# A Hymba-style encoder block with a hierarchical MoE on one core: the scatter of the pair before moves behind this pair's up matmuls

## The reference

```python
# 4 groups x 8 experts, d_model 1024, d_expert 512, all float32
h = h + mix @ w_o[l]
h = h + hier_moe(rms_norm(h, norm2_g[l]), w_group[l], b_group[l], w_expert[l], b_expert[l],
                 w_gate[l], w_up[l], w_down[l])
return rms_norm(h, final_g)
...
# hier_moe: top-1 group, then top-2 experts in it; combine holds the weight of each token and expert
for gi in range(N_GROUPS):
    h = jax.nn.silu(jnp.einsum('nd,edf->nef', xt, w_gate[gi])) * jnp.einsum('nd,edf->nef', xt, w_up[gi])
    y = y + jnp.einsum('nef,efd->nd', h * combine[:, gi, :, None], w_down[gi])
```

## Time and profile before

| what | value |
|---|---|
| runs | 638.72 us median of 3 (636.98 to 640.76) |
| profiled execution, span | 639.8 us; no time beside the span is given for it, and it lies within the runs |
| TensorE matmul busy | 593.8 us, 93% |
| TensorE weight load busy | 288.1 us, 45% |
| VectorE / ScalarE / GpSimd busy | 149.8 / 77.6 / 28.5 us |
| mean granted TensorE clock | 0.982 of full speed |
| read from HBM | 216.16 MB, 340 GB/s over the span |

### The profile page before, as it was taken

The page is one execution under the profiler, slowest core; times in us unless marked ns, Lnnn a source line. Parts: engine busy times, 40 slices in busy tenths (PEclk is TensorE's granted clock), DMA queues, the critical chain, the costliest instruction groups (busy, mean ns, idle before and its releaser), DMA issues.

```text
span 639.8 us, 6965 instructions
## 1 busy us (share of the span) xinstructions
PE 593.8 (93%) x2801; PEld 288.1 (45%) x2801; DVE 149.8 (23%) x331; ACT 77.6 (12%) x151; POOL 28.5 (4%) x60
## 2 busy tenths in 40 slices
PE   4999899959999999999999999999999999999984
PEld 2445657546535353544434343434353535344321
DVE  1006545251111111121213031211111111212023
ACT  2013323121000010101000101010000101010002
POOL 2031200210000000000000000000000000000001
PEclk9999989978999999999999999999999999999999
DMA  6995680073989999999999999999999999979701
GB/s 259 338 425 226 248 288 1 34 296 130 385 349 419 416 413 410 411 421 416 419 413 418 411 419 420 414 420 417 417 415 419 421 410 410 410 296 392 307 1 67
DMA packets 35939, 217.50 MB, mean 340 GB/s; under 512 B 5136, under 2 KB 6184, under 8 KB 28368
## 3 DMA queue, kind: packets, MB, share of 16 engines
q1 hardware_dynamic: 31680, 214.30, 82.3%
q10 hardware_dynamic: 4240, 2.94, 1.4%
HBM read 216.16 MB, written 1.06 MB: 340 GB/s over the span
## 4 chain that ended last, share of the span: by engine, by line
PE 91%; DVE 5%; issue 2%; DMA 1%; SPq 0%; ACT 0%; POOLq 0%; POOL 0%; DVEq 0%; ACTq 0%
PE bank L1188 33%; PE bank L1216 17%; PE bank L1175 10%; PE bank L1226 10%; PE bank L1003 7%; PE bank L1072 4%; PE bank L1062 2%; PE bank L1267 2%; DVE region_x L882 2%; PE bank L986 2%; PE bank L1040 1%; PE bank L1282 1%; PE bank L1051 1%; DMA ring<-in_norm_g_dram 1%; DVE region_q L886 1%
## 5 line engine op out<-in xcount | busy, mean ns | idle before, releaser
L1188 PE MATMUL bank<-ring,region_x 128*64 128x512 f32 x960 | 212.1, 594 | 0.6 <-issue 0.6
L1188 PEld LDWEIGHTS bank<-ring,region_x 128*64 128x64 f32 x960 | 75.0, 137 | 132.5 <-issue 132.5
L1216 PE MATMUL bank<-ring,region_q 128*64 128x512 f32 x480 | 106.3, 594 | 15.3 <-DVE region_q L886 8.7
L897 DVE TENSOR_TENSOR h<-h,bank 128x512 f32<-128x512 f32 x64 | 44.0, 687 | 238.2 <-PE bank L1226 238.2
L1216 PEld LDWEIGHTS bank<-ring,region_q 128*64 128x64 f32 x480 | 39.7, 137 | 72.2 <-issue 72.2
L1175 PEld LDWEIGHTS bank<-region_q,region_t 128*128 128x128 f32 x512 | 61.0, 199 | 14.0 <-issue 14.0
L1175 PE MATMUL bank<-region_q,region_t 128*128 128x128 f32 x512 | 64.0, 285 | 1.7 <-DVE region_q L878 1.7
L1226 PE MATMUL bank<-region_x,region_q 128*128 128x512 f32 x128 | 62.2, 618 | 0.7 <-ACT region_x L621 0.7
L1003 PE MATMUL bank<-ring,region_x 128*128 128x512 f32 x96 | 44.7, 622 | 0.8 <-DVE region_x L660 0.8
L1226 PEld LDWEIGHTS bank<-region_x,region_q 128*128 128x128 f32 x128 | 20.4, 188 | 42.4 <-DVE h L897 21.0
L621 ACT ACTIVATE region_x<-bank 128x512 f32<-128x512 f32 x32 | 19.1, 597 | 159.3 <-PE bank L1216 140.3
(11 more groups left out here) (156 smaller groups left out, 273.5 us busy)
## 6 DMA issues: line engine op xcount, KB each, us to landing
ring<-in_w_gate_dram SPq DMA_DIRECT2D x30, 2048.0 KB, 12.3
ring<-in_w_up_dram SPq DMA_DIRECT2D x29, 2048.0 KB, 12.2
ring<-in_w_down_dram SPq DMA_DIRECT2D x29, 2048.0 KB, 11.9
ring<-in_w_in_dram SPq DMA_DIRECT2D x8, 768.0 KB, 9.1
ring<-in_w_up_dram SPq DMA_DIRECT2D x12, 512.0 KB, 9.7
ring<-in_w_down_dram SPq DMA_DIRECT2D x12, 512.0 KB, 9.2
ring<-in_w_o_dram SPq DMA_DIRECT2D x2, 2048.0 KB, 8.6
ring<-in_w_gate_dram SPq DMA_DIRECT2D x8, 512.0 KB, 7.8
```

Of the source, the lines that this page charges most:

```text
L897: dve.tensor_tensor(part, part, ps[SC0 + k % 2][:], ALU.add).then_inc(sc_free, 1)
L1188: last = pe.matmul(ps[bank][64 * a:64 * a + 64, :], xgT[:, c, 64 * a:64 * a + 64], slots[s][:, c * F:(c + 1) * F], start=(c == 0), stop=(c ...
L1216: last = pe.matmul(ps[GD0 + half][64 * a:64 * a + 64, :], hT[:, c, 64 * a:64 * a + 64], w[:, c * D + 512 * half:c * D + 512 * half + 512], ...
```

## The change

On TensorE, a step's order becomes: gather of i (now in two calls of `gather_half`), pick transposes (`turn_picks`), down of i-1, gate of i, up of i, scatter of i-1, transposes of i. The transposes of a pair's activations thus stand at the end of the step before the one with its down; those of pair 0 follow its up ahead of the first step. The wait for the two gather copies ahead of down is split: the first half of down waits for ScalarE's, the second for VectorE's. On VectorE, the hT copy goes ahead of the GD1 copy, and the product ahead of the four adds. ScalarE's and SyncE's programs are unchanged.

```diff
@@ VectorE
             def pair_step(trip, j):
                 i = trip * BODY + (1 + j)
+                hT_out(trip * BODY + j)
                 gathered_out(i)
-                hT_out(trip * BODY + j)
                 dve.wait_ge(picks_turned, i + 1)
                 make_picks(trip * BODY + (2 + j), trip * BODY + (base + j + 1))
+                product(i)
                 add_outputs(trip * BODY + j)
                 places_out(i)
-                product(i)
...
+            hT_out(PAIRS - 2)
             gathered_out(PAIRS - 1)
-            hT_out(PAIRS - 2)
+            product(PAIRS - 1)
             add_outputs(PAIRS - 2)
             places_out(PAIRS - 1)
-            product(PAIRS - 1)
             hT_out(PAIRS - 1)
             add_outputs(PAIRS - 1)
@@ TensorE
-            def gather(i):
-                pe.wait_ge(pick_ready, i + 1)
-                for b in range(2):
-                    for c in range(4):
-                        for t in range(TT):
-                            last = pe.matmul(ps[GD0 + b][:, c * P:(c + 1) * P], hn[:, t, 4 * b + c, :], pick[:, t, :],
-                                             start=(t == 0), stop=(t == TT - 1))
-                    last.then_inc(gathered, 1)
+            def gather_half(i, b):
+                if b == 0:
+                    pe.wait_ge(pick_ready, i + 1)
+                for c in range(4):
+                    for t in range(TT):
+                        last = pe.matmul(ps[GD0 + b][:, c * P:(c + 1) * P], hn[:, t, 4 * b + c, :], pick[:, t, :],
+                                         start=(t == 0), stop=(t == TT - 1))
+                last.then_inc(gathered, 1)
+
+            def turn_picks(i):
                 if not isinstance(i, int) or i > 0:
                     pe.wait_ge(place_ready, i)
                 for t in range(TT):
...
-            def down(i, trip, f):
+            def down(i, trip, f, after):
                 pe.wait_ge(hT_ready, i + 1)
                 landed(pe, trip, f + 4)
                 landed(pe, trip, f + 5)
                 for half in range(2):
+                    pe.wait_ge((xg_act, xg_dve)[half], after + 1)
                     for c in range(FC):
...
-            gather(0)
+            gather_half(0, 0)
+            gather_half(0, 1)
+            turn_picks(0)
             products(0, 0, FIRST_FILL, GATE, gate_done, gate_pieces)
             products(0, 0, FIRST_FILL + 2, UP, up_done)
             pe.wait_ge(first_pieces_in, 16 * 2 * (PIECES - 1))
             pe.nop().then_inc(scattered, 4)
+            turn_act(0)
...
-                gather(i)
-                turn_act(before)
-                pe.wait_ge(xg_act, i + 1)
-                pe.wait_ge(xg_dve, i + 1)
-                down(before, trip, f - 6)
+                gather_half(i, 0)
+                gather_half(i, 1)
+                turn_picks(i)
+                down(before, trip, f - 6, i)
                 return i, before, f
 
             def whole_pair_step(trip, j):
                 i, before, f = pair_step(trip, j)
                 products(i, trip, f, GATE, gate_done)
+                products(i, trip, f + 2, UP, up_done)
                 scatter(before)
-                products(i, trip, f + 2, UP, up_done)
+                turn_act(i)
...
             last_product(0, GATE, gate_done)
+            last_product(1, UP, up_done)
             scatter(PAIRS - 2)
-            last_product(1, UP, up_done)
             turn_act(PAIRS - 1)
```

## The result

The changed kernel takes 618.37 us, the median of 4 runs (616.26 to 621.16), against 639.74 for the one before on the same chip: a ratio of 0.966 (0.963 to 0.970), 21 us less. The forecast was 622.2, with a range from 618.5. The direction and the bound are right; the gain is larger than the 16.6 us of the sum, and the median lies just under the range. What failed in the sum is the price of the gather in its new place, and in a small part that of down; this is taken up behind the experiments.

A forecast was written before the change was run, and what follows sets the result against it. TensorE's order of work was taken as the bound, idle between gather and down. Steps of 29.09 for 30.23 us gave 14.8, minus 0.2 first, plus 2.05 last: 16.6 less, 622.2 us median; own range 619.5 to 625.

The forecast's parts named there:

- the sum: Whole kernel: 14.8 us gained in thirteen steps, 0.2 lost in the first, 2.05 gained in the last; 16.6 less.
- the price of the gather in its new place: TensorE, each step: the gather was entered at 3.78 us in the step sum of 29.09.
- bounds for down: TensorE, down behind a pick transpose: between 6.87 and 7.09 us, entered at 7.09.
- shows no such seam: TensorE, gate to scatter: a second seam would give 0.15 us and a 28.94 step; left out of the sum.
- The low end of the range: Whole kernel: 619.5 us as own range, step 28.95; below it 618, with down at 6.87 and a shorter scatter.
- the 1.75 forecast: Last step, after the scatter: down waits 1.75 us for hT, behind the last add and L902 on VectorE.
- A: TensorE's transposes cost 0.67 and the sequencer's 0.34 stays ahead of down: 0.57 us a step, 630 us; chance 0.12.
- B: VectorE's product delays the scatter's adds if over 0.29 us later: 627 us at half its 0.69, 632 at all; chance 0.10.
- D: VectorE's hT copy comes late for down, beyond 2.6 us of margin: slower, 653 us at 4.8 us delay; chance 0.02.
- C: Weight loads set the pace as the ring runs short: 625 or 630 us, L273 standing for microseconds; chance 0.10.
- E: Loads already fill the step, idle time moves to L273: only the last step's 2.05 us gained, 636.7 median; chance 0.03.
- L273's 51 ns: Median wait for landed weights, taken as evidence against loads setting the pace; expected to stay at 51 ns.

The follow-up runs named there:

- third-bank version: The changed kernel with the scatter's third matmul writing the bank GATE, so only the fourth waits for an add of this pair: 615.58 us, ratio 0.961; again 615.44, 0.960.
- adds-first run: The changed kernel with VectorE's product behind the four adds and the copy L902, as before the change: 648.04 us, ratio 1.011.
- hT run: The changed kernel with VectorE's hT copy behind its GD1 copy, as before the change: 639.92 us, ratio 1.000.
- half-gather run: The changed kernel with the second block of 128 tokens left out of the gather, same loads: 609.87 us, ratio 0.954.
- product-late run: The kernel before, with only VectorE's product of a pair moved behind its GD1 copy for the next pair: 673.11 us, one run.

## Where the prediction was right, and the step of it that failed

**The bound** was read rightly: TensorE's order, with the idle place at down. The gap is now 0.22 as forecast, the transposes take 0.44, and the scatter 3.82. Four things had to be right at once for a step of 28.80. Each was taken back in a run of its own, and these are the prices a step: the split wait 0.8, hT ahead of the GD1 copy 1.3, the product ahead of the adds 1.9, the scatter as cover 1.2.

**The step that failed** is the pricing of the gather and of down in their new places. The prediction took the gather over at its 3.78, though it moved from behind up to behind transposes. The runs: the gather takes 3.78 behind up, with or without the product beside it, and 3.57 to 3.59 behind a scatter or transposes (but for the six of 3.65 to 3.71). That is 0.21 a step. Of its bounds for down, 6.87 and 7.09, the prediction took the upper. Down takes 7.02 behind running work and 7.09 only behind an idle time, another 0.07. Together they are what the step was short of, 29.09 - 28.80 = 0.29, in thirteen steps 3.8 us. With 0.2 in the first step and 0.3 in the last, the sum of 16.6 becomes 20.9, against 21.0 in the traces. The mechanism of the gain held; it was these two terms that had the wrong size.

**Why the gather's term was missed.** The seams are changes between 64-column and 128-column matmuls. Before, a step had four: ahead of down, of the scatter, of up and of the gather. The new order takes away those ahead of up (0.15) and of the gather (0.21). The prediction named only the first. It looked for the second ahead of the scatter, where the trace "shows no such seam", though in its own words the scatter stands behind a 64-column stream as before; the one that goes is the gather's. The rows of the gather's weight loads in the pages of the kernel before and of the changed one show it too, 14.0 us of idle time ahead of them for 1.9:

```profile
L1175 PEld LDWEIGHTS bank<-region_q,region_t 128*128 128x128 f32 x512 | 61.0, 199 | 14.0 <-issue 14.0
...
L1175 PEld LDWEIGHTS bank<-region_q,region_t 128*128 128x128 f32 x512 | 59.8, 196 | 1.9 <-issue 1.9
```

The two seams that stay have a price as well. Ahead of the scatter it is 0.20 by the third-bank version; that was measured behind up, and that it is as much behind gate follows only from the 3.82 that the scatter takes in either place. It moved with the scatter and changes no sum. Ahead of down it can be read from down's 7.02 against gate's 6.87, for as many records. The Trainium skill, TensorEngine Tiling (Array Packing), Key Properties, says that a change of tiling mode drains TensorE; the 3.78 and 3.57 of the gather, the 7.02 and 6.87 of up and the 3.63 of the scatter agree with it.

**Slips in the working.** The low end of the range was built on down at 6.87 and a scatter without 0.4 us of waits. These are 0.22 and 0.4 a step, 14 x 0.62 = 8.7, and would have put it near 613.5; the text takes 0.3 a step, half of it, and gives no reason. A step of 28.95 belongs to a time of some 620.3, not 619.5. Six of the thirteen steps before, not one in three, took 30.15; the sum, which goes by their mean, doesn't hang on that.

**First and last step.** The first took 30.29 for 30.49: 0.28 less by the gather and down, 0.09 more since the bare transposes of pair 0 hold up the gather by 1.49 and not 1.4. The last took 30.08 for 30.40, by the same 0.28; its wait for hT came out nearly as priced:

```profile
594.71 0.42 DVE region_q L902
595.12 0.61 DVE region_q L886
...
595.78 7.11 PE bank L1288 x32
```

The scatter ends at 594.08 and down starts 1.70 later, for the 1.75 forecast.

**The rivals.** A, dearer seams, went the other way: transposes behind the scatter cost 0.44. B would have needed 0.29 us: that is what VectorE idles between product and add, so the cover holds exactly as thin as priced. The adds-first run shows the price when the order on VectorE is wrong, larger than the 0.69 that I gave as the most for B, since there the transposes wait for all of the queue. D didn't come: hT is ready 2.6 us ahead of down. What a late hT costs is shown by the hT run, which loses just what the gain was. C was closer than its chance of 0.10 says. The loads do fall back 1.0 a step; by the estimates above the ring has some 20 us, and 13 of them are used. E, next to no gain, is ruled out by thirteen steps that are 1.43 shorter, with no wait for a transfer in them.

**A piece of evidence that was none.** I leaned on L273's 51 ns for saying that no transfer is waited for, and named it as the sign of C. In the half-gather run the loads hold up TensorE for 14 us, and L273 still stands at 51 ns: the wait shows only as idle time of L1190 with a DMA as its releaser. The conclusion for the kernel before stands on the chain and on the releasers, not on this row.

## What to carry to other kernels

Price a moved block by the row of the same work behind the neighbour that it will have, not behind the one that it has: the same 32 records took 3.78 or 3.57 by what ran ahead of them, and a seam can hide in another wait. A new order on one engine is worth what the queues of the others make of it; here one exchanged pair of lines on VectorE took back all of 21 us, another made a loss of it. Where a ring lets the loads fall back for a while, read how far they fall per step and how many steps are left, since a longer loop, or the next gain on the compute side, meets that limit.

## What the runs showed of the hardware

TensorE's granted clock could fall to the lower level behind a short idle time, and not each time. Stretches of 2.96 to 3.11 us with TensorE busy for 0.86 of them stood ahead of the 15 downs of the product-late run: eight of these downs took some 8.78 us (mean granted clock 0.81), seven took 7.09 (1.00), and the length of the stretch didn't decide which. In the half-gather run TensorE did nothing at all for 2.56 to 2.59 us ahead of four ups; two took 8.78 at 0.81, two 7.09 at 1.00. The gaps of 1.6 to 1.7 us in the kernel before cost nothing of the kind: all 15 downs took 7.09.

The weight stream of this one core moved 420 to 424 GB/s in each of twelve steps of the changed kernel, from 191 to 537 us, and 421 over 400 us of the half-gather run; before the change twelve of the thirteen steps had 411 to 418.
